# The first mixer's opening reordered: gate projection before head 0's scores, half of head 1's values before head 0's state product

## The reference, cut to what matters

```python
q, k, v, r, lr = jnp.split(proj, [GLA_DK, 2 * GLA_DK, 2 * GLA_DK + GLA_DV, 2 * GLA_DK + 2 * GLA_DV], axis=-1)
gk = jax.nn.log_sigmoid((lr @ w_gk2 + b_gk).astype(f32)) / GLA_GATE_NORMALIZER
b = jnp.cumsum(gc, axis=2)
q_in = qc * jnp.exp(b - b_mid)
k_in = kc * jnp.exp(b_mid - b)
scores = jnp.where(causal, jnp.einsum('bcihd,bcjhd->bchij', q_in, k_in), 0.0)
q_inter = qc * jnp.exp(b)
k_state = kc * jnp.exp(b_last[:, :, None] - b)
# per chunk: o_i = q_inter @ state; state = state * exp(b_last) + k_state^T v
o = rmsnorm(o_intra + o_inter, g_norm) * silu(r)
return o @ w_out
```

## Time and profile before

| what | value |
|---|---|
| median of 3 runs | 1169.73 us (1167.99 to 1170.42) |
| profiled execution, its own time | 1166.21 us |
| its span, first to last instruction | 1164.5 us |
| mean granted TensorE clock | 0.979 of full speed |
| share of PE in the chain that ended last | 88% |
| PE busy | 1111.0 us, 95% |
| weight loads on PE busy | 947.5 us, 81% |
| DVE busy | 733.4 us, 63% |
| ACT busy | 631.9 us, 54% |
| bytes over the span | 199.24 MB, 171 GB/s |

### The profile page before, as it was taken

How to read it: one execution, slowest core, us unless ns; L and a number is a source line. 1 busy time by engine, 2 the same in 40 slices (tenths; PEclk the granted TensorE clock), 3 DMA queues, 4 the chain that set the end, 5 groups by cost and what they waited for, 6 DMA issues and landing times.

```text
span 1164.5 us, 16442 instructions
## 1 busy us (share of the span) xinstructions
PE 1111.0 (95%) x5868; PEld 947.5 (81%) x5868; DVE 733.4 (63%) x1170; ACT 631.9 (54%) x984; POOL 54.1 (5%) x81
## 2 busy tenths in 40 slices
PE   6899999969989999999999997999999989999997
PEld 5788888868968888888888885889999977888886
DVE  4555545656587555457655545598999978655553
ACT  6444444665367444447544444576776776544443
POOL 3000000000000000000000000221122100000000
PEclk9899999989999999999999999899999989999999
DMA  7756554444446565554756534484555424765530
GB/s 249 253 181 211 172 173 129 127 145 145 145 142 226 192 215 176 171 195 129 246 185 210 173 100 148 134 283 148 160 160 164 145 72 159 258 216 180 172 116 37
DMA packets 162877, 199.24 MB, mean 171 GB/s; under 512 B 6372, under 2 KB 145856, under 8 KB 162832
## 3 DMA queue, kind: packets, MB, share of 16 engines
q1 hardware_dynamic: 160144, 190.34, 50.4%
q0 software_dynamic: 2384, 7.72, 1.9%
q10 hardware_dynamic: 304, 0.61, 0.1%
HBM read 197.56 MB, written 1.08 MB: 171 GB/s over the span
## 4 chain that ended last, share of the span: by engine, by line
PE 88%; DVE 6%; ACT 3%; issue 1%; DMA 1%; SPq 0%; DVEq 0%; ACTq 0%
PE ps L1414 41%; PE ps L1433 25%; PE ps L1466 8%; PE ps L1476 6%; PE ps L1425 2%; PE ps L1775 1%; DVE ws L918 1%; DVE ws L1000 1%; PE ps L1456 1%; ACT ws L530 1%; DMA raw<-in_ffn_w_down 1%; PE ps L1584 1%; DVE xT L990 1%; DVE xres L966 0%; DVE ca L1191 0%
## 5 line engine op out<-in xcount | busy, mean ns | idle before, releaser
L1414 PE MATMUL ps<-ws,xT 128*128 128x512 f32 x2160 | 502.4, 391 | 6.2 <-DVE ws L1000 6.2
L1414 PEld LDWEIGHTS ps<-ws,xT 128*128 128x128 f32 x2160 | 404.9, 188 | 93.7 <-DVE ws L1000 8.0
L1433 PE MATMUL ps<-ws,hT 128*128 128x512 f32 x1344 | 335.2, 400 | 4.0 <-DVE hT L1291 3.9
L1433 PEld LDWEIGHTS ps<-ws,hT 128*128 128x128 f32 x1344 | 251.5, 191 | 57.5 <-issue 5.9
L1000 DVE TENSOR_TENSOR ws<-raw,ws 128x1024 fp32r<-128x1024 f32 x180 | 218.2, 1223 | 115.8 <-ACT ws L590 115.8
L918 DVE TENSOR_TENSOR ws<-raw,ws 128x2048 fp32r<-128x2048 f32 x90 | 206.4, 2293 | 98.1 <-ACT ws L530 97.7
L590 ACT ACTIVATE ws<-raw 128x1024 fp32r<-128x1024 f32 x180 | 188.4, 1061 | 144.9 <-PE ps L1414 139.8
L530 ACT ACTIVATE ws<-raw 128x2048 fp32r<-128x2048 f32 x90 | 171.0, 1913 | 62.7 <-PE ps L1433 57.1
L1466 PE MATMUL ps<-xT,ws 128*128 128x256 f32 x960 | 119.3, 284 | 0.3 <-ACT feat L536 0.3
L1466 PEld LDWEIGHTS ps<-xT,ws 128*128 128x128 f32 x960 | 116.4, 192 | 0.9 <-issue 0.9
L1476 PE MATMUL ps<-ws,xT 128*128 128x256 f32 x672 | 88.3, 292 | 0.4 <-ACT ca L536 0.3
(11 more groups left out here) (211 smaller groups left out, 613.0 us busy)
## 6 DMA issues: line engine op xcount, KB each, us to landing
raw<-in_ffn_w_down SPq DMA_DIRECT2D x88, 512.0 KB, 4.4
raw<-in_ffn_w_gate SPq DMA_DIRECT2D x86, 512.0 KB, 4.0
raw<-in_ffn_w_up SPq DMA_DIRECT2D x86, 512.0 KB, 5.0
raw<-in_ssd_w_in SPq DMA_DIRECT2D x48, 512.0 KB, 4.7
raw<-in_gla_w_in SPq DMA_DIRECT2D x24, 512.0 KB, 4.7
raw<-in_ssd_w_out SPq DMA_DIRECT2D x16, 512.0 KB, 4.5
raw<-in_gla_w_out SPq DMA_DIRECT2D x8, 512.0 KB, 4.7
exps<-cs_rows POOLq DMA_DIRECT2D x8, 512.0 KB, 8.5
```

The lines of the kernel that those rows point to most:

```text
L1414: mm = pe.matmul(ps[:, bank + t, :].rearrange("p (s n) -> p s n", s=2), xT[:, k, a, t * P:(t + 1) * P], ws[:, 0:2, b, k * UW:(k + 1) * UW] ...
L1433: mm = pe.matmul(ps[:, 2 * t + n, :], hT[:, par, j, a, t * P:(t + 1) * P], ws[:, slot, b, off:off + 512], start=(first and j + a + b == 0) ...
```

## The change

It has five parts, all of them in the GLA mixer.

1. **Gate logits earlier.** On PE the two transposes of `RPRE` move into the middle of the pair, and the four logit matmuls move in front of head 0's q and k. On DVE the low half of `SLOT_P1` (head 1) moves behind the absolute value.
2. **Decay chain.** ACT does Ln straight after Exp and copies head 0's q and k out behind it; then it makes the high half of `SLOT_P3` (head 1's values), which stood in `body(1)`. `decayed` for head 0 waits for each exponential by itself and no more for all of them.
3. **PE's order in body(1).** Head 1's gate goes into banks 0 and 1, in front of head 0's `rows` and scores. `token_tiles(SLOT_P3, 2, (0,))`, the first 128 tokens of head 1's values, stands in front of head 0's state product, the second 128 tokens behind the state matmul; both go into banks 2 and 3. `open_banks` goes: the first `down_half` of head 0 starts its banks itself and waits for `p3_out` of 4 in `body(2)`.
4. **DVE and ACT in body(1).** DVE copies the state first and makes the low half of `SLOT_P1` (head 2) after it. ACT makes the high half of `SLOT_O` behind the copies of the values.
5. **No hardware loop** for the GLA heads on PE, ACT and DVE: `body(2)` is written out.

```diff
@@ gla_start on ACT
                 act.activation(et, et, ACT.Exp, scale=-1.0).then_inc(gla_act, 1)
-                tiles_out(SLOT_P3, n0[SLOT_P3], 2, [ca[:, c, :] for c in range(2)], p1_out)
                 act.wait_ge(gla_act, 1)
                 act.activation(et, et, ACT.Ln, bias=1.0).then_inc(gla_act, 1)
+                tiles_out(SLOT_P3, n0[SLOT_P3], 2, [ca[:, c, :] for c in range(2)], p1_out)
+                hi(SLOT_P3, n0[SLOT_P3] + 1)
...
@@ body on ACT
                     if proj:
-                        hi(SLOT_P3, g + n0[SLOT_P3])
-                        tiles_out(SLOT_P2, g + n0[SLOT_P2], A,
+                        if paired_first:
+                            act.wait_ge(zs_done, 1)
+                        else:
+                            hi(SLOT_P3, g + n0[SLOT_P3])
+                        tiles_out(SLOT_P2, g + n0[SLOT_P2], 0 if paired_first else A,
...
-                    if scan:
+                    if scan and not paired_first:
                         hi(*out_unit(g - 1, n, n0))
...
+                    if paired_first:
+                        hi(*out_unit(g - 1, n, n0))
...
@@ gla_start on DVE
                 dve.tensor_tensor(lrT, lrT, ps[0:GLA_RANK, E, 0:T], ALU.mult).then_inc(lr_scaled, 1)
-                lo(SLOT_P1, n0[SLOT_P1] + 1)
...
                 dve.scalar_tensor_tensor(out=et, in0=z, scalar=-1.0, in1=z, op0=ALU.mult, op1=ALU.max).then_inc(gla_dve, 1)
+                lo(SLOT_P1, n0[SLOT_P1] + 1)
                 lo(SLOT_P2, n0[SLOT_P2] + 1)
...
-                dve.wait_ge(gla_act, 7)
-                decayed(0, 0, (2, 0, 1, 3))
+                for o, exponentials in ((2, 4), (0, 5), (1, 6), (3, 7)):
+                    dve.wait_ge(gla_act, exponentials)
+                    decayed(0, 0, (o,))
...
@@ body on DVE
-                    if proj and not ahead:
+                    if proj and not ahead and not paired_first:
                         lo(SLOT_P1, g + n0[SLOT_P1] + 1)
                     if scan:
                         if not ssd:
                             dve.wait_ge(upd_mm, g)
                             dve.tensor_copy(st[:, 0, :], ps[:, E, 0:256]).then_inc(state_done, 1)
+                    if paired_first:
+                        lo(SLOT_P1, g + n0[SLOT_P1] + 1)
...
@@ gla_start on PE
                     small(GLA_RANK, ph)
+                    pe.wait_ge(r_done, NT * ph + 2)
+                    for t in range(NT):
+                        mm = pe.transpose(ps[0:GLA_RANK, E, t * P:(t + 1) * P], RPRE[t].broadcast_to([P, GLA_RANK]), ident[:, :])
+                    mm.then_inc(r_row, 1)
                 first_pair(ph, low_rank)
...
-                split(SLOT_P3, n0[SLOT_P3])
-                pe.wait_ge(post_read, 4 * ph)
-                feature_tiles(SLOT_P3, 2, (0,))
                 pe.wait_ge(lr_scaled, 1)
...
                 mm.then_inc(gla_mm, 1)
-                feature_tiles(SLOT_P3, 2, (1,))
+                split(SLOT_P3, n0[SLOT_P3])
+                pe.wait_ge(post_read, 4 * ph)
+                feature_tiles(SLOT_P3, 2)
...
@@ body on PE
+                        opens = not ssd and o == 0
+                        if opens:
+                            pe.wait_ge(p3_out, 4)
                         for t in tiles:
-                            down_half(slot, par, t, 0, last=last)
+                            down_half(slot, par, t, 0, first=opens, last=last)
...
+                    if paired_first:
+                        split(SLOT_P2, g + n0[SLOT_P2])
+                        pe.wait_ge(p2_out, 2)
+                        pe.wait_ge(p3_out, 2)
+                        token_tiles(SLOT_P2, 0)
                     if scan and proj:
 
                         pe.wait_ge(feat_done, 4 * (g - 1 + G) + (2 if ssd else 4))
                         pe.wait_ge(p3_out, 2 * (g - 1 + G) + 2)
                         rows(g - 1)
-                    if proj:
+                    if proj and not paired_first:
...
-                        if first and not ssd:
-                            open_banks()
...
+                    if paired_first:
+                        split(SLOT_P3, g + n0[SLOT_P3])
+                        token_tiles(SLOT_P3, 2, (0,))
                     if scan:
...
+                        if paired_first:
+                            pe.wait_ge(w_done, 2)
+                            pe.wait_ge(p1_out, c0 + 2)
...
+                    elif paired_first:
+                        token_tiles(SLOT_P3, 2, (1,))
```

More of the change, by code:

```diff
@@ L39 @@
 SSD_WEIGHTS = 4
-SSD_STEPS, GLA_STEPS = 15, 17
+SSD_STEPS = 15
 MASKED_FIRST = 2
@@ L114, in pipeline @@
     body(1, True, True, False)
-    with eng.Fori(2, n - 1) as g:
-        body(g, True, True, True)
+    if n == GLA_H:
+        for g in range(2, n - 1):
+            body(g, True, True, True)
+    else:
+        with eng.Fori(2, n - 1) as g:
+            body(g, True, True, True)
     body(n - 1, True, True, True)
@@ L786, in body @@
                     first = isinstance(g, int) and g == 1
+                    paired_first = first and not ssd
                     ahead = isinstance(g, int) and g == n - 1
@@ L887, in body @@
                     elif proj:
-                        tiles_out(SLOT_P3, g + n0[SLOT_P3], C, [(zf if ssd else vs)[:, t, :] for t in range(2)], p3_out,
+                        tiles_out(SLOT_P3, g + n0[SLOT_P3], 2 if paired_first else C,
+                                  [(zf if ssd else vs)[:, t, :] for t in range(2)], p3_out,
                                   (1.0, 1.0) if ssd else [R2[:, t:t + 1] for t in range(2)])
+                    if paired_first:
+                        hi(*out_unit(g - 1, n, n0))
                 pipeline(act, n, body)
@@ L1383, in mixer @@
                 body(1, True, True, False)
[L1384 to L1388, removed]
+                if ssd:
+                    with dve.Fori(2, n - 1) as g:
+                        step.body(g, 2, SSD_STEPS)
+                        body(g, True, True, True)
+                    step.after(n - 3, SSD_STEPS)
+                else:
+                    for g in range(2, n - 1):
+                        body(g, True, True, True)
                 body(n - 1, True, True, True)
@@ L1714, in add_output @@
                         par = 1 if isinstance(o, int) and o == n - 1 else 0
+                        opens = not ssd and o == 0
+                        if opens:
+                            pe.wait_ge(p3_out, 4)
                         for t in tiles:
-                            down_half(slot, par, t, 0, last=last)
+                            down_half(slot, par, t, 0, first=opens, last=last)
                             if last and t == 1:
                                 x_transposed(ph + 1, 0)
-                            down_half(slot, par, t, 1, last=last)
+                            down_half(slot, par, t, 1, first=opens, last=last)
                     if outp and (proj or not scan):
@@ L1754, in body @@
                             pe.wait_ge(e_out, g)
-                        if not ssd:
+                        if not ssd and not paired_first:
                             pe.wait_ge(w_done, 2 * (g - 1 + G) + 2)
```

4 lines of the change are left out of this document (removed).

## The result

The changed kernel takes 1151.08 us, the median of four runs (1150.72 to 1152.56), beside 1168.86 for before (four runs, 1167.63 to 1170.42). The ratio is 0.985 with a 95% interval of 0.9833 to 0.9867, a gain of 17.8 us in these medians. The profiled execution took 1151.12 with a span of 1149.4, which is 15.1 less than the span before. So three figures are to be told apart, 14.0, 15.1 and 17.8.

A forecast was written before the change was run, and what follows sets the result against it. PE bounds the kernel, pausing 8.96 us in the GLA mixer's opening: pause 8.96, clock 2.0, zero matmuls 1.0, two waits 1.95, slow short groups about 1, less 0.9 new waits, gain 14.0: 1155.7 us, range 1153.0 to 1159.2.

The forecast's parts named there:

- opening in all: PE from the low-rank product's start to head 0's transposes, GLA mixer: the whole gain, 14.0 us, was forecast here.
- What bounds the kernel: PE, busy 95% of the span; in the GLA mixer's opening it waits 8.96 us for DVE's last `decayed` tile.
- the cover of 1.7 us: Before `rows`: head 1's gate keeps PE busy to 246.35, when `fm` has been ready for 1.7 us.
- DVE as the next to be late: Before head 2's q and k: DVE's product with the gate ends at 255.6, so PE waits 0.8 us.
- the end of PE's slow gate: Head 1's gate: its 48 matmuls take 5.94 us at full clock, not 7.97; 2.0 us of gain from the clock.
- The loop's price of 0: Hardware loop of the GLA heads: its removal gains 0, with bounds 0 to 0.2 us.
- the chain did not slip: Rival, before `rows`: decay chain 3 to 4 us later, PE waits about 2, gain 12, 1157.7 us; chance 0.12.
- PE kept 2.4 GHz in the opening: Against the rival that short pauses hold PE at 1.2 GHz in parts: gain 11, 1158.7 us; chance 0.05.
- DVE's lateness: Rival, at head 2: PE pays DVE's 4.2 us, gain 9.8, 1159.9 us, chance 0.09; at all three heads, 1168.3, chance 0.03.
- The load of head 1's values: Rival "slower", decay chain: the load decides from a landing at 237; landing after 255 gives 1172.2 us or more; chance 0.03.
- the step from the sum to the time: Whole kernel: profiled 1166.21 becomes 1152.2; the median's 3.5 us excess is carried over, 1169.7 - 14.0 = 1155.7.
- the clock read from one window: Window at 330 to 340: PE idle 2.04 of 10 us, granted 1.00, so the stretch from 240 runs at 2.4 GHz.

The follow-up runs named there:

- first pair of traces: Profiles of the kernel before and the changed kernel: 1166.21 and 1151.12 us, from low-rank product to head 0's transposes 54.43 and 40.17.
- second trace of before: The kernel before, unchanged, run again as a kernel of its own: traced execution 1166.36 us at a mean granted clock of 0.979.
- filled kernel: Kernel before plus 32 zero matmuls in PE's 8.96 us pause: 1164.98 us beside 1167.67, ratio 0.9986; its traced execution took 1169.05.
- other order: Changed kernel with all 48 matmuls of head 1's values behind head 0's state matmul: 1151.68 us, ratio to before 0.9854.
- two halves of this change: Kernel before with parts 1, 2 (without the moved high half), loop written out: 1163.09 us; with parts 3, 4, moved high half, loop written out: 1160.50.

## Why the prediction was right or wrong, point by point

In this table the marks of the profile after are shifted by 2.70 us, by which its low-rank product began earlier than in the profile before (218.36 against 221.06). The shift arose in the first feed-forward stage.

| step of the prediction | forecast | measured, shifted |
|---|---|---|
| logit matmuls begin | 226.7 | 226.9 |
| L1144 (now L1156) begins | 236.1 | 236.2 |
| last exponential ends | 244.0 | 244.0 |
| `fm` complete | 244.6 | 244.6 |
| `rows` begins | 246.35 | 246.2 |
| state product | 250.3 | 250.0 |
| second half of the values | 251.85 | 251.5 |
| head 2's q and k | 255.6 | 255.15 |
| wait in front of head 0's transposes | 0.1 | 0.3, with the hand-over |
| opening in all | 14.0 shorter | 14.05 shorter (14.26 in the first pair of traces) |

**Right.** What bounds the kernel, parts 1 to 4, the cover of 1.7 us, DVE as the next to be late, and the end of PE's slow gate all came out within half a microsecond. The loop's price of 0 stands. Of the rivals none came: the chain did not slip, PE kept 2.4 GHz in the opening, and from head 2 on PE showed none of DVE's lateness (the next body's q and k follow at 278.61, 26.16 later, as before at 26.07). The load of head 1's values was never waited for.

**Wrong: the step from the sum to the time.** It said that the profiled execution stands 3.5 below the median and that this difference is carried over, and that below 1153 only a gain above 16.7 would come. In the changed kernel the profiled execution (1151.12) stands at the median (1151.08): the term of 3.5 measured 0. The other 1.1 of the miss of 4.6 is that the profiled execution took 1151.12 and not 1152.2: it was 2.7 ahead at the opening, gained 0.26 more in it and lost 1.8 behind it. Seen from the means of all runs, the same 4.6 are three terms that the step left out:
- The median of before, 1169.73 from three runs, was itself 1.5 above the mean of 74.
- 2.0 came outside the opening, most likely from the clock there. I had taken the clock to matter only where the change acts, and had fixed the rest of the run as it stood in one trace.
- The median of four runs of the changed kernel was 1.1 below its mean of 13.

The bounds for these lay open. The three runs of before spread over 2.4 us, and the trace was 3.5 from their median: that scatter belonged into the range at both ends, about 2 us on each.

**Wrong: the clock read from one window.** The prediction took the earlier trace rows as evidence that PE with 2 us of pauses in 10 keeps its clock. It also read the 2.04 us as several waits: 1.93 of them are one, in front of 335.53. The same work was granted 0.84 in the second trace of before and 0.83 in the profile after, and pauses of 1.68 and 0.45 in the filled kernel were followed by a gate at 0.77 (252 to 259). What was forecast for the opening held, with a pause of about 0.6 left in it; but so did the clock in before over the waits of 0.62 and 1.33 (1.00 from 258.3 to 270), so these runs name no length that is safe.

**Half right: what the half in front is for.** The prediction counted its cover and its lateness both, and had the change as a whole. It did not ask what the other order would give. Measured, the cover is worth 0.33 and the lateness costs 0.9 to 1.

## What to carry to other kernels

When a long pause of PE is closed, close it wholly: with 4.10 or 3.20 us of the 8.96 left, the clock behind was lost here all the same, and the two halves of this change brought 3.4 and 7.9 us alone but 14.05 together. A forecast from one trace can hold to 0.1 us where the change acts and still miss the time, so take the scatter of the runs and the pauses elsewhere into the range. Where PE must wait for 1.5 to 6 us, matmuls that nobody reads, in a free bank and ahead of the wait, were worth 7 to 9 us in this run of 1150; behind the wait, 15 of them added 2.9.

## What was not expected of the hardware

- The granted clock behind pauses of 1.5 to 6 us differs from run to run of one program: 1.00 in the first trace of before and 0.84 in the second for the same 10 us of work, and a mean from 0.973 to 0.980 over the runs of before, with times from 1164.7 to 1170.8.
- Matmuls with zeros held the clock: with 32 of them it was 1.00 through a stretch (242 to 249.5) that in before was a pause, granted 0.75 (240.5 to 249.5).
- A table load between Exp and Ln costs 1.28 us, with at most 0.02 between it and its neighbours (231.09 to 231.11, 232.39 to 232.41), even where ACT has nothing else to do.
